# In the last pair, sixteen rows of the first weight chunk are loaded by two transfers of eight rows, the other 112 rows by one

## What is computed

```python
def moe_ffn(h, w_router, b_router, w_up, b_up, w_down, b_down):
    logits = (ht @ w_router + b_router)
    top_val, top_idx = lax.top_k(logits, TOP_K)
    gates = jax.nn.softmax(top_val, axis=-1)
    ...
    def expert_block(args):
        e, tok, gate = args
        hu = h_pad[tok] @ w_up[e] + b_up[e]
        x_glu, x_lin = jnp.split(hu, 2, axis=-1)
        x_glu = jnp.minimum(x_glu, SWIGLU_LIMIT)
        x_lin = jnp.clip(x_lin, -SWIGLU_LIMIT, SWIGLU_LIMIT)
        act = x_glu * jax.nn.sigmoid(SWIGLU_ALPHA * x_glu) * (x_lin + 1.0)
        return (act @ w_down[e] + b_down[e]) * gate[:, None]
```

## Time and profile before

| | |
|---|---|
| median of three runs | 1034.05 us |
| the profiled execution, its time | 1034.71 us |
| its span, first to last instruction | 1032.6 us |
| PE busy / weight loads / DVE / ACT | 97% / 38% / 20% / 11% |
| DMA moved | 424.98 MB, 412 GB/s on the mean |
| granted TensorE clock, mean | 0.995 |

### The profile page before, as it was taken

One profiled execution on the slowest core, in us unless ns is written; L12 is line 12 of the kernel. 1 busy time (PEld: TensorE's weight loads), 2 busy tenths in 40 slices (PEclk: granted clock), 3 DMA queues, 4 the chain that ended last, 5 costly groups with the idle time before them and its releaser, 6 DMA issues.

```text
span 1032.6 us, 10869 instructions
## 1 busy us (share of the span) xinstructions
PE 1006.2 (97%) x4512; PEld 394.3 (38%) x4512; DVE 202.8 (20%) x486; ACT 114.5 (11%) x231; POOL 12.8 (1%) x26
## 2 busy tenths in 40 slices
PE   9999999999999999999999999899998999999998
PEld 6446553433343434333333334242433334342432
DVE  0556132121111211212121211112111211112012
ACT  2427101010000000010101000000000000100001
POOL 0200000000000000000000000000000000000000
PEclk9999999999999999999999999999999999999999
DMA  9965999999999999999999999999999999999996
GB/s 362 414 249 239 386 352 430 425 402 425 427 431 434 432 429 433 434 432 429 433 434 432 429 432 435 430 430 430 435 430 430 434 432 430 430 435 425 428 428 273
DMA packets 23619, 424.98 MB, mean 412 GB/s; under 512 B 3728, under 2 KB 4496, under 8 KB 7472
## 3 DMA queue, kind: packets, MB, share of 16 engines
q1 hardware_dynamic: 23216, 424.18, 96.8%
q10 hardware_dynamic: 384, 0.54, 0.2%
HBM read 423.65 MB, written 1.05 MB: 411 GB/s over the span
## 4 chain that ended last, share of the span: by engine, by line
PE 64%; DMA 32%; SPq 2%; another core or an unknown queue 1%; DVE 1%; issue 0%; ACT 0%; POOLq 0%; POOL 0%; DVEq 0%
DMA everything<-in_w_moe 31%; PE psum L1446 27%; PE psum L1486 14%; PE psum L1102 4%; PE psum L1366 3%; PE psum L1327 3%; PE psum L1235 3%; PE psum L1064 2%; SPq L491 2%; PE psum L1317 2%; PE psum L1077 1%; PE psum L1094 1%; DMA everything<-in_b_down 1%; PE psum L1085 1%; PE psum L1375 0%
## 5 line engine op out<-in xcount | busy, mean ns | idle before, releaser
L1446 PE MATMUL psum<-everything 128*64 128x512 f32 x2048 | 463.7, 598 | 1.2 <-DMA everything<-in_w_moe 0.9
L1486 PE MATMUL psum<-everything 128*64 128x512 f32 x1024 | 233.4, 606 | 19.5 <-DMA everything<-in_w_moe 19.5
L1446 PEld LDWEIGHTS psum<-everything 128*64 128x64 f32 x2048 | 138.1, 136 | 294.5 <-issue 286.8
L1486 PEld LDWEIGHTS psum<-everything 128*64 128x64 f32 x1024 | 76.2, 139 | 163.2 <-issue 161.7
L743 DVE TENSOR_TENSOR everything<-psum,everything 128x512 f32<-128x512 f32 (+1 forms) x38 | 25.0, 663 | 350.2 <-PE psum L1327 333.1
L1029 DVE TENSOR_SCALAR everything<-psum 128x512 f32<-128x512 f32 x32 | 22.1, 692 | 337.4 <-PE psum L1446 337.4
L1327 PEld LDWEIGHTS psum<-everything 128*128 128x128 f32 x480 | 55.8, 191 | 24.3 <-issue 24.3
L1366 PE MATMUL psum<-everything 128*128 128x512 f32 x126 | 63.5, 606 | 0.2 <-DMA everything<-in_w_moe 0.2
L696 ACT ACTIVATE everything<-everything 128x512 f32<-128x512 f32 x32 | 20.2, 631 | 383.9 <-DVE everything L1029 383.9
L1327 PE MATMUL psum<-everything 128*128 128x128 f32 x480 | 61.5, 281 | 0.0
L1102 PE MATMUL psum<-everything 128*128 128x512 f32 x96 | 42.1, 594 | 0.0
(11 more groups left out here) (164 smaller groups left out, 304.1 us busy)
## 6 DMA issues: line engine op xcount, KB each, us to landing
everything<-in_w_moe SPq DMA_DIRECT2D x78, 4096.0 KB, 42.0
everything<-in_w_moe SPq DMA_DIRECT2D x29, 2048.0 KB, 17.8
everything<-in_w_moe SPq DMA_DIRECT2D x11, 1024.0 KB, 9.4
everything<-in_w_in SPq DMA_DIRECT2D x3, 2048.0 KB, 25.9
everything<-in_w_out SPq DMA_DIRECT2D x2, 2048.0 KB, 11.1
everything<-in_w_moe SPq DMA_DIRECT2D x6, 512.0 KB, 33.9
everything<-in_w_mem_kv SPq DMA_DIRECT2D x1, 2048.0 KB, 16.8
everything<-in_w_in SPq DMA_DIRECT2D x3, 512.0 KB, 7.3
```

What stands on the lines that cost most here:

```text
L1446: mm = pe.matmul(psum[r:r + SLOTS, bank], XT[:, k, r:r + SLOTS], weights[i][:, column:column + N], start=k == 0 and not (first and j < hal ...
L1486: mm = pe.matmul(psum[r:r + SLOTS, DOWN_BANKS[n]], actT[:, 2 * i + k, r:r + SLOTS], slot[:, column:column + N], start=i == 0 and k == 0, s ...
```

## The change

In `last_pair`, chunk 0 is no longer loaded by one transfer of 128 rows. One transfer takes rows 0 to 111 and adds to `two_in[0]`; two further transfers take rows 112 to 119 and 120 to 127. Those two add to the router's semaphore, renamed `router_and_rest_in`, and PE waits for 16 + 32 on it before it uses the chunk. By the description of the change the transfers of eight rows go through eight DMA engines. The bytes are the same, and no other chunk and no other pair is touched.

```diff
-            sp.dma_start(wr, w_router[0].rearrange("(k p) e -> p k e", p=P)).then_inc(router_in, 16)
+            sp.dma_start(wr, w_router[0].rearrange("(k p) e -> p k e", p=P)).then_inc(router_and_rest_in, 16)
...
                         arrived = (odd_in if j % 2 else two_in)[j // 2],
+                    if j == 0:
+
+                        rows = P - 2 * 8
+                        sp.dma_start(slots[j][0:rows], src[0:rows]).then_inc(two_in[0], 16)
+                        for r in range(rows, P, 8):
+                            sp.dma_start(slots[j][r:r + 8], src[r:r + 8]).then_inc(router_and_rest_in, 16)
+                        continue
                     size = SLOT_COLS // len(arrived)
...
-            pe.wait_ge(router_in, 16)
+            pe.wait_ge(router_and_rest_in, 16)
...
                 elif j % 2 == 0:
                     pe.wait_ge(two_in[j // 2], q * 16 + 16 * (TWO_LOADS[j // 2] - 1))
+                    if last and j == 0:
+                        pe.wait_ge(router_and_rest_in, 16 + 2 * 16)
```

More of the change, by code:

```diff
@@ L297, in layer_kernel @@
             sem("const_in"), [sem("x_in0"), sem("x_in1")], [sem("mem_in0"), sem("mem_in1")])
-        pos_in, params_in, router_in = sem("pos_in"), sem("params_in"), sem("router_in")
+        pos_in, params_in, router_and_rest_in = sem("pos_in"), sem("params_in"), sem("router_and_rest_in")
         xT_in, memT_in = [sem(f"xT_in{i}") for i in range(len(FIRST_PIECES) - 1)], sem("memT_in")
```

## The result

The changed kernel takes 1041.59 us (median of six runs, 1039.59 to 1044.59) against 1033.94 us for the kernel before (six runs, 1033.36 to 1034.72). The ratio is 1.0075 with a 95% interval of 1.0061 to 1.0088: **7.7 us slower**, 6.3 to 9.1 by the interval. The forecast of no change is wrong, and the time lies 3 us above the range. The profiled execution took 1041.20 us with a span of 1039.0 us, 6.4 us longer than the span before.

The account below looks back on a forecast made before the run. The prediction took the weight stream's last landing plus 8.8 us as the bound. Balance of -0.6 or +0.6 us, taken as 0, plus 0.1 for small transfers gave 1034.0 us from 1034.05; range 1033.2 to 1038.6.

Parts of the forecast that it names:

- What bounds the kernel: At the kernel's end: the landing of the last weight quarter plus 8.8 us of untouched work sets the time.
- The bound on the gain: In the DMA run-out after 1019.5 us: any redistribution between the engines can give at most 2.2 us, 0.21%.
- Term 1: Chunk 0's 112-row transfer: dealt over 16 engines, each has one row less, -0.61 us.
- Term 2: Chunk 0's two 8-row transfers: one row per engine each on eight engines, +1.22 us on those eight.
- Term 3: Cost of the two small transfers beyond their bytes: between 0 and 0.63 us, taken as 0.1.
- Term 4: Two more DMA issues on SP before chunk 1's: 0.7 us in all, covered by the queue, cost 0.
- term 5: PE's additional wait before the last pair's first product: chunk 0 lands 4.6 us before its use, cost 0.
- its reserve of 2.44 us: PE's idle time at the last quarters' weight loads: PE may be delayed that much earlier without moving the end.
- Crowding: Rival, chance 0.36: engines writing neighbouring partitions share a memory entrance in the 8-row transfers; middle +3.7 us, 1037.8 us.
- The fetch: Rival, chance 0.06: the run-out's 16 KB instruction fetch moves off the late engine, landing up to 1.2 us earlier, 1032.3 us.
- theory A: On-chip memory partitions lie in groups of four neighbours behind 16 entrances, and engines writing behind one of them share it.

Follow-up runs that it names:

- experiment 3: The changed kernel without its two 8-row transfers (rows 112 to 127 not loaded), against the kernel before: +5.3 us by the medians, ratio 1.0043.
- experiment 1: Chunk 0 of the last pair cut by columns into three transfers of the same sizes, each 128 rows high, against the kernel before: +0.3 us, ratio 1.0005.
- experiments 4 to 7: Chunk 0 as two 64-row transfers, against the kernel before: neighbouring rows +6.5 us; even/odd +0.8; even/odd read, halves written +5.8; halves read, even/odd written -0.2.
- Experiments 6 and 7: Two 64-row transfers, against the kernel before: even/odd rows read and written to partition halves, +5.8 us; halves read and written to even/odd partitions, -0.2 us.

## Why the prediction was wrong, point by point

**What bounds the kernel: right.** The landing of the last quarter moved from 1023.84 to 1030.33, by 6.5 us, and the span by 6.4. The bound on the gain, 2.2 us in the run-out, stood on a sound reading too. It was a bound on one side only.

**Term 1, the 112 rows, is the step that failed.** It was put at -0.61 us, one row less for each engine. It costs +5 to +6 us (experiment 3). The sum took "dealt evenly" for "as fast as before". It counted what each engine carries, and not where each engine writes. The rival text named the point in half a sentence, "112 rows may fall on the entrances unevenly too, up to some us more", and then didn't price it.

**Term 2, the dealing, was right and of no use.** Eight engines do carry the small transfers (packet counts). Whether the balance moved the end by 0.6 us, and which way, can't be told beside 7.7 us.

**Term 3, the small transfers: mis-sized.** 0.1 us taken, 0.63 as the bound; 1.5 to 3 us by difference. The row chosen as nearest, the b_up transfers of the earlier trace rows, was not near. They are 2 KB a row, an eighth of a weight row, so even a crowded one had little to crowd with. A small loss measured on short rows doesn't bound the loss on rows eight times as long. That those two were put nearer to 0 because their rows are as long as the chunks' was no sound reason: if the loss is a share of the time that the bytes take, long rows make it larger. No run here varies the length of a row.

**Term 4, SP's issues, and term 5, PE's wait as such: right** (experiment 1, +0.3 us). PE did come to wait 3.28 us at its first product: chunk 0's last rows landed at 976.60 instead of 968.8, 7.8 us later, and its cover was 4.6. But its reserve of 2.44 us at the quarters and the later quarters covered it.

**The rivals.** Crowding, at 0.36, is what happened, by the sign, the place (the dip around 965 us) and the dependence on target partitions. It forecast 1035.9 to 1039.5, and 1041.6 came, as it had only the two small transfers in its price, and these turned out cheaper than the 4.3 to 5.5 us that it gave them. So its mechanism fits the runs, and most of the loss came from where it had no price. The page of the Trainium skill that was cited for it, "SBUF — State Buffer", section "Door 1: The DMA port swizzle", agrees with experiments 4 to 7: 64 neighbouring partitions, which by it lie behind 8 of 16 ports, lose 6.5 us, and 64 even ones, which lie behind all 16, lose nothing. The trace confirms a size only for single rows, which take twice as long in the rows four apart, and not for the totals. By 8 ports the two halves would lose 4.9 us, and the 16-row transfers come out closer together than 4 and 8 ports would have them. The mistake was to weigh the rule lower than a row of the trace that didn't test it. The fetch didn't move: in the changed kernel, too, one instruction fetch of 16 KB falls into the run-out (at 1026.51 us, before at 1019.21).

**What stays open.** How 112 rows are dealt to the engines isn't visible in any view, so why they run at about half rate is argued from theory A and not shown. A bare count wouldn't give it: with 128 partitions behind 16 entrances no entrance has more than eight rows of the transfer, with 112 rows as with 128. It must be that several engines are at one entrance at the same time while another is free, and no run isolates that for 112 rows. Experiments 6 and 7 exclude the reading side for the halves only. Nor is it shown how one engine's delay passes to the others, which is where the simple count of entrances fails in size. A dealing that relieves the late engines without crowding wasn't tried. By theory A it might not exist: if each engine of a full-height transfer has partitions behind an entrance of its own, a row given to another engine still needs the same entrance.

## What to carry to other kernels

Where the stream of weights is the bound, cut transfers by columns and keep all 128 partitions, or take every second one (transfers of 16 partitions eight apart lost 7 us here, of eight partitions four apart 11); not a block of neighbouring partitions, even if the counts of rows, bytes and engines come out even: blocks of 8, 16, 64 and 112 all lost time. Before moving work between engines, read from the run-out how much there is to gain (here 2.2 us of 1034) and hold it against what a disturbed transfer costs (here half the rate for the length of a chunk). And price the part of a change that seems untouched: here 112 of 128 rows that only got shorter by an eighth cost more than the 16 that were the point.

## What the runs showed of the hardware that was not expected

A 2 MB load of 64 + 64 rows costs 6.5 us more when each transfer writes neighbouring partitions, and nothing when it writes every second one. The DMA engines' busy share doesn't show it (1.04, 1.07 and 1.00 in the changed kernel's slow stretches); only the rate does. The time is also less even: the six runs of the changed kernel spread over 5.0 us and the four of 112 + 16 rows over 6.5, those of the kernel before over 1.4 us. Not every crowded kernel shows it (112 rows alone: 2.6 us).
